# Experts in four units of columns, down parts between the units, and seven products in place of eight in two units' gates

## The chip, the core and the metric

One core of a Trainium2 chip runs the kernel. The metric is the time of one execution on the device in microseconds (us); less is better. TensorE (PE; its weight loads are PEld), VectorE (DVE), ScalarE (ACT), GpSimd (POOL) and SyncE (SP) run side by side and wait for one another through semaphores. DMA engines bring weights from HBM to SBUF, and the DMAs of one queue are served in the order of issue.

## The reference

A two-layer encoder for 256 tokens of width 1024, float32. Each layer has a mixer (a gated linear recurrence and a dilated attention) and a feed-forward part; the first layer's is a dense SwiGLU, the second's has eight experts of which each token uses two:

```python
def moe_swiglu(h, w_router, w_gate, w_up, w_down):
    logits = (h @ w_router).astype(jnp.float32)
    top_val, top_idx = lax.top_k(logits, TOP_K)
    top_w = jax.nn.softmax(top_val, axis=-1)
    combine = jnp.sum(jax.nn.one_hot(top_idx, N_EXPERTS, dtype=jnp.float32) * top_w[..., None], axis=-2)
    out = jnp.zeros(h.shape, jnp.float32)
    for e in range(N_EXPERTS):
        y = swiglu(h, w_gate[e], w_up[e], w_down[e]).astype(jnp.float32)
        out = out + combine[..., e:e + 1] * y
    return out.astype(h.dtype)
```

`swiglu` is `(silu(h @ w_gate) * (h @ w_up)) @ w_down`. Gate and up matrices are 1024 x 3584, the down matrix is 3584 x 1024, per expert. The eight experts' weights are 352 MB.

## The kernel before

Up to about 650 us the kernel does the mixers, the dense layer and the routing; the change leaves that alone. Then come the experts, one after the other, e = 0 to 7. For each, 96 places (`CAP`) hold the tokens that chose it, in three groups (`GROUPS_E`) of 32 (`STRIP`). The gathered rows, transposed, are `gT` (two buffers, by the parity of e); the next expert's rows are fetched by an indirect DMA of POOL into `fetched` and transposed by VectorE (`turn_fetched`).

**TensorE.** The token groups are the stationary operand, 32 columns wide, so four products run at once in four lanes of 32 columns of the array; a weight matrix's rows stream through. float32 products take two passes, and each pass is recorded as one weight load and one multiply, so a product has four records. The gate and up matrices are cut into two units (`UNITS_E`) of 1792 columns, 448 (`LANE_W`) per lane. A *part* is one load: for gate and up 128 rows by 1792 columns (896 KB, 12 products of 448 columns, L1508), 32 parts in an expert; for the down matrix 256 rows by 1024 columns (1024 KB, L1536), 14 parts. `E_ORDER` lists the 46 parts; the down parts come last. Gates are summed in three banks (`early`), ups in three others (`late`), the down products in `turn[0]`, `turn[1]` and `late[2]`.

**Seven products in place of eight.** In experts 0 to 6 (`seven`), two of the three token groups and each down part are treated as 2 x 2 blocks: with sums of weight blocks t1 to t4 (`sums_a`, `sums_w`, four sets, `SETS`) and sums of token blocks s1 to s4 (`xn`), seven products do the work of eight. With the third group's four, a down part has 11 products instead of 12. VectorE makes the sums: one operation of 1024 columns (t1 and t3, L2135), one of 512 (t2, "third sum", L2140, semaphore `w_second`), one of 512 (t4, "fourth sum", L2124, `w_sums`). TensorE waits for `w_second` before a down part and for `w_sums` within it. Expert 7 has the plain 12 products (L1570, L1582; of its last three parts the products into `turn[1]` come after those into `turn[0]`).

**VectorE in an expert.** Adding up the previous expert's rows and choosing the next one's (about 13 us); gating of unit 0 (L2219: up times SiLU of the gate; L2223: transposes into `hT`; L2110 to L2115: the token sums), the transposes of the next rows (L2099), the sums of the first three down parts (`AHEAD`), which stand behind a wait for those parts to land; gating of unit 1, and the sums of the other eleven. ScalarE takes the SiLU of a unit's gates (L1145).

**Loads.** SP issues one DMA per part (L742). The experts' parts go through a ring of 11 places (`RING`: `wide`, ten places that are partly `raw` before, and `extra`). Part m is asked for when part m-11 has been used. The first ten are asked for before the experts start, the eleventh (L738) when the gathered tokens are stored.

## Time and profile before

| what | value |
|---|---|
| median of 3 runs | 1529.07 us (1528.86 to 1533.36) |
| profiled execution | 1528.53 us |
| its span (first to last instruction) | 1526.7 us |
| TensorE busy | 1508.6 us, 99% |
| VectorE busy | 921.5 us, 60% |
| ScalarE busy | 497.4 us, 33% |
| HBM, read and written | 476 MB, 312 GB/s over the span |
| granted TensorE clock | 0.998 of 2.4 GHz |

The page cuts the span into 40 slices of 38.2 us; a digit is the busy share in tenths. The experts begin in the eighteenth slice. A busy TensorE isn't a TensorE at its peak, since a multiply's record covers its way through the array too; the pace is better read from the starts of pieces in the chain, the list of work that ended last. "DMA to landing" is the time from the issue of a load to the moment its semaphore is complete.

### The profile page before, as it was taken

How to read it: one execution, taken by the hardware profiler on the slowest of the kernel's cores; microseconds unless marked ns; L12 is line 12 of the kernel's file. 1: busy time of each engine (PE TensorE's matmuls, PEld its weight loads, DVE VectorE, ACT ScalarE, POOL GpSimd, SP SyncE). 2: the span in 40 equal slices, each digit the busy share in tenths (PEclk: the TensorE clock that was granted, in tenths of full speed). 3: DMA queues.
4: the chain of work that ended last, by engine and by line, in shares of the span. 5: the costliest groups of instructions: out<-in, count | busy, mean ns of one | idle time of the engine just before them, and what ended most of it. 6: DMA issues, size and time to landing. Idle time of an engine off the chain costs nothing.

```text
span 1526.7 us, 27999 instructions
## 1 busy us (share of the span) xinstructions
PE 1508.6 (99%) x11888; PEld 1033.6 (68%) x11888; DVE 921.5 (60%) x1533; ACT 497.4 (33%) x741; POOL 25.3 (2%) x39
## 2 busy tenths in 40 slices
PE   9999999999999999999999999999999999999997
PEld 7887788888888878843466566565565665664664
DVE  7778776888787776643824835726528339248211
ACT  5698745444457987420020110100100100201001
POOL 0000000000000000010000000000000000000100
PEclk9999999999999999999999999999999999999999
DMA  9544376555554444499999999999999999999994
GB/s 385 177 162 164 116 248 207 186 184 182 194 179 149 155 166 146 141 364 425 425 410 425 425 417 425 418 416 425 418 420 426 413 425 424 412 425 416 422 425 183
DMA packets 72673, 478.10 MB, mean 313 GB/s; under 512 B 8097, under 2 KB 8353, under 8 KB 45154
## 3 DMA queue, kind: packets, MB, share of 16 engines
q1 hardware_dynamic: 68656, 460.09, 75.8%
q0 software_dynamic: 3456, 15.72, 2.7%
q8 instruction: 97, 1.59, 0.4%
q10 hardware_dynamic: 434, 0.45, 0.1%
q14 instruction: 30, 0.25, 0.0%
HBM read 471.38 MB, written 4.85 MB: 312 GB/s over the span
## 4 chain that ended last, share of the span: by engine, by line
PE 85%; ACT 6%; DVE 5%; DMA 2%; issue 1%; SPq 0%; ACTq 0%; DVEq 0%
PE bank L1508 24%; PE mid L1508 12%; PE turn L1536 11%; PE bank L1233 7%; PE bank L1239 7%; PE bank L1242 7%; PE mid L1536 4%; PE mid L1233 2%; PE mid L1239 2%; PE mid L1242 2%; PE turn L1570 2%; ACT w_hi L586 1%; DVE w_lo L593 1%; DMA wide<-in_e_down 1%; PE mid L1345 1%
## 5 line engine op out<-in xcount | busy, mean ns | idle before, releaser
L1508 PE MATMUL bank<-wide,gT 128*32 128x448 f32 x3624 | 438.5, 539 | 0.0
L1508 PEld LDWEIGHTS bank<-wide,gT 128*32 128x32 f32 x3624 | 221.4, 110 | 131.6 <-issue 22.6
L593 DVE TENSOR_TENSOR w_lo<-raw,w_hi 128x1024 fp32r<-128x1024 f32 x202 | 244.4, 1223 | 93.0 <-ACT w_hi L586 90.6
L1508 PE MATMUL mid<-wide,gT 128*32 128x448 f32 x1824 | 254.2, 539 | 0.0
L586 ACT ACTIVATE w_hi<-raw 128x1024 fp32r<-128x1024 f32 (+1 forms) x202 | 210.2, 1053 | 101.1 <-PE bank L1242 65.5
L1145 ACT ACTIVATE eh<-bank 128x448 f32<-128x448 f32 x48 | 22.6, 544 | 478.3 <-PE bank L1508 478.3
L1536 PE MATMUL turn<-wide,hT 128*32 128x512 f32 x534 | 176.8, 592 | 1.4 <-DVE sums_w L2140 1.4
L1233 PE MATMUL bank<-w_hi,a_hi 128*128 128x512 f32 (+1 forms) x608 | 164.6, 394 | 0.8 <-ACT a_hi L869 0.8
L2219 DVE TENSOR_TENSOR eh<-mid,eh 128x448 f32<-128x448 f32 x32 | 19.8, 620 | 241.2 <-PE mid L1508 241.2
L1508 PEld LDWEIGHTS mid<-wide,gT 128*32 128x32 f32 x1824 | 115.5, 110 | 66.4 <-issue 12.8
L1242 PE MATMUL bank<-w_lo,a_hi 128*128 128x512 f32 (+1 forms) x608 | 157.1, 381 | 2.1 <-DVE w_lo L593 2.1
L1239 PE MATMUL bank<-w_hi,a_lo 128*128 128x512 f32 (+1 forms) x608 | 157.7, 383 | 0.0
L1536 PE MATMUL mid<-wide,hT 128*32 128x512 f32 x498 | 137.7, 592 | 0.0
L1242 PEld LDWEIGHTS bank<-w_lo,a_hi 128*128 128x128 f32 x608 | 111.3, 188 | 25.1 <-DVE w_lo L593 2.9
L1239 PEld LDWEIGHTS bank<-w_hi,a_lo 128*128 128x128 f32 x608 | 111.9, 189 | 22.7
L1233 PEld LDWEIGHTS bank<-w_hi,a_hi 128*128 128x128 f32 x608 | 109.4, 189 | 22.7 <-ACT a_hi L869 1.2
L1536 PEld LDWEIGHTS turn<-wide,hT 128*32 128x32 f32 x534 | 54.6, 109 | 56.1 <-issue 30.4
L1536 PE MATMUL turn<-wide,xn 128*32 128x512 f32 x178 | 91.1, 593 | 0.0
L2135 DVE TENSOR_TENSOR sums_a<-wide 128x1024 f32<-128x1024 f32 x49 | 59.8, 1220 | 49.8 <-DMA wide<-in_e_down 49.7
L1113 ACT ACTIVATE yt<-mid 32x512 f32<-32x512 f32 x7 | 4.1, 585 | 262.5 <-PE mid L1536 262.5
L2135 DVE TENSOR_TENSOR sums_w<-wide 128x1024 f32<-128x1024 f32 x40 | 48.8, 1220 | 47.9 <-DMA wide<-in_e_down 47.9
L1536 PEld LDWEIGHTS mid<-wide,hT 128*32 128x32 f32 x498 | 46.5, 110 | 25.2 <-issue 2.5
(313 smaller groups left out, 1985.0 us busy)
## 6 DMA issues: line engine op xcount, KB each, us to landing
wide<-in_e_in SPq DMA_DIRECT2D x227, 896.0 KB, 12.4
wide<-in_e_down SPq DMA_DIRECT2D x102, 1024.0 KB, 13.6
raw<-in_stream SPq DMA_DIRECT2D x100, 1024.0 KB, 4.8
extra<-in_e_in SPq DMA_DIRECT2D x23, 896.0 KB
extra<-in_e_down SPq DMA_DIRECT2D x10, 1024.0 KB
raw<-in_e_in SPq DMA_DIRECT2D x6, 896.0 KB, 4.5
wg<-in_gates POOLq DMA_DIRECT2D x2, 2048.0 KB, 10.5
table<-y_rows POOLq DMA_DIRECT2D x7, 384.0 KB
```

The lines of the kernel that those rows point to most:

```text
L586: nc.scalar.activation(w_hi[:, h % H, 0:n], raw[:, part % R, lo:lo + n], ACT.Copy).then_inc(hi_ready, 1)
L593: nc.vector.tensor_tensor(w_lo[:, h % H, :], raw[:, part % R, lo:lo + HALF], w_hi[:, h % H, :].bitcast(F32), ALU.subtract).then_inc(lo_rea ...
L1145: nc.scalar.activation(eh[t_][:, :], early[t_][:, 0:LANE_W], ACT.Silu).then_inc(e_silu, 1)
L1233: nc.tensor.matmul(o_, s_hi[:, kt, t], w_hi[:, h % H, w], start=kt == 0, stop=False)
L1239: nc.tensor.matmul(o_, s_lo[:, kt, t], w_hi[:, h % H, w], start=False, stop=False)
L1242: ins = nc.tensor.matmul(o_, s_hi[:, kt, t], w_lo[:, h % H, w], start=False, stop=kt == last_kt)
L1345: ins = nc.tensor.matmul(mid[:, q, g * T:(g + 1) * T], wg[:, d, g, n, :], xc[:, n, :], start=True, stop=True)
L1508: ins = nc.tensor.matmul((early, late)[m][t_][strip(r), 0:LANE_W], gT[:, kt, strip(t_)], w_[:, r * LANE_W:(r + 1) * LANE_W], start=kt == 0 ...
L1536: return nc.tensor.matmul(bank_[strip(lane), :], h_, b_, start=d == from_, stop=d == to)
L1570: ins = nc.tensor.matmul(turn[0][strip(s_), :], h_[:, c * CAP + STRIP * t_: c * CAP + STRIP * (t_ + 1)], w_c, start=first and c == 0, stop ...
L2135: nc.vector.tensor_tensor(own_[:, 0:2, :], blocks[:, :, 1, :], blocks[:, 0, :, :], ALU.subtract).then_inc(w_first, 1)
L2219: nc.vector.tensor_tensor(eh[t_][:, :], late[t_][:, 0:LANE_W], eh[t_][:, :], ALU.mult).then_inc(e_hid, 1)
```

## The change

- Columns: four units of 1024, 1024, 1024 and 512 columns (`WIDTHS` = 256, 256, 256, 128 per lane). Every part is now 1024 KB: two blocks of 128 rows by 1024 columns, or in unit 3 four blocks of 128 rows by 512. An expert has 28 gate and up parts and 14 down parts, 42 loads in place of 46, from one tensor `e_parts`.
- Order in an expert (parts counted from 0): unit 0 (0 to 7), unit 1 (8 to 15), down parts of unit 0 (16 to 19), unit 2 (20 to 27), down of unit 1 (28 to 31), unit 3 (32 to 35), down of unit 2 (36 to 39), down of unit 3 (40, 41). In units 0 to 2 two gate parts, two up parts, two gate parts, two up parts.
- Gates of units 1 and 2 in experts 0 to 6 have seven products in place of eight for two token groups: 28 products of 128 columns and, for the third group, 8 of 256. The other parts have 24 products of 256 columns; in unit 3 they have 48 of 128.
- The weight sums of these 8 gate parts per expert are made by VectorE like those of the down parts, in the same four sets and with the same lead of three parts: 22 parts in place of 14. The seven gate products are then combined: ScalarE copies two of them out of PSUM, VectorE makes five additions (`combine_gate`), ScalarE takes the SiLU of the result. Four more operations of 128 columns per expert sum the gathered rows (`gathered_sums`).
- VectorE's program in an expert follows the parts: in step i the sums of part i+3, the fourth sum of a part behind the first of the next; the combination and the gating of a unit at the step in which its last gate or up part has been used; the transposes of the next rows in steps 9, 10 and 11.
- The products of the ups use `late[0]` and `late[1]` only, so `late[2]`, `turn[0]` and `turn[1]` are taken by the down products from part 16 on.

```diff
-UNITS_E = 2
-LANE_W = F_EXP // (UNITS_E * LANES)
+WIDTHS = (256, 256, 256, 128)
+UNITS_E = len(WIDTHS)
+LANE_W = WIDTHS[0]
+SEVEN_UNITS = (1, 2)
...
+    return unit(0) + unit(1) + down(0) + unit(2) + down(1) + unit(3) + down(2) + down(3)
...
+                        act.wait_ge(used, u0 + GATE_END[u] + e * E_PARTS)
+                        if split:
+                            k = len(SEVEN_UNITS) * e + SEVEN_UNITS.index(u)
+                            nc.scalar.activation(part_sum[:, 0, :], early[0][:, 0:P], ACT.Copy).then_inc(gate_copied, 1)
+                            nc.scalar.activation(part_sum[:, 1, :], early[1][:, 2 * P:3 * P],
+                                                 ACT.Copy).then_inc(gate_copied, 1)
...
+                                four(early[0][:, 0:P], a11, b11, opens=True)
+                                four(early[0][:, P:2 * P], a12, b21)
+                                four(early[1][:, 0:P], s4, b22, opens=True)
+                                pe.wait_ge(w_second, n + 1)
+                                four(early[1][:, 3 * P:4 * P], s3, t3)
+                                four(early[1][:, 2 * P:3 * P], s1, t1)
+                                four(early[0][:, 2 * P:3 * P], s2, t2, closes=True)
+                                pe.wait_ge(w_sums, n + 1)
+                                four(early[1][:, P:2 * P], a22, t4, closes=True).then_inc(w_sums_used, 1)
...
+                        for i in range(E_PARTS):
+                            if i in UP_END or i in GATE_END and GATE_END.index(i) in SEVEN_UNITS:
+                                if owed is not None:
+                                    fourth_sum(e, owed)
+                                    owed = None
+                                if i in UP_END:
+                                    gating(e, UP_END.index(i))
+                                else:
+                                    combine_gate(e, GATE_END.index(i))
+                            if 9 <= i < 9 + GROUPS_E:
+                                turn_fetched(e, [i - 9])
+                            if i + AHEAD in SEVENS:
+                                first_sums(e, i + AHEAD)
+                                if owed is not None:
+                                    fourth_sum(e, owed)
+                                third_sum(e, i + AHEAD)
+                                owed = i + AHEAD
+                                if i + 1 + AHEAD not in SEVENS:
+                                    fourth_sum(e, owed)
+                                    owed = None
```

`four` issues one product of 128 columns in each of the four lanes.

TensorE before, in expert 0, from the end of the third down part to the fourth and into the fifth (`turn0`, `turn1` and `mid` are the down sums, `xn` the token sums, `part_landed` a load's semaphore, `weight_sums_third` is `w_second`, `weight_sums_ready` is `w_sums`):

```order
L1536 MATMUL turn0<-sums_w,hT 32x512 [waits weight_sums_ready]
L1536 MATMUL mid<-wide,hT 32x512 x2
L1536 MATMUL turn0<-wide,hT 32x512 [waits weight_sums_third,part_landed1]
L1536 MATMUL turn1<-sums_w,xn 32x512 x2
L1536 MATMUL turn0<-sums_w,xn 32x512
L1536 MATMUL turn1<-wide,hT 32x512
```

TensorE after, in expert 0, from the end of the down parts of unit 0 into the first gate part of unit 2 and to the next one (`gS` holds the sums of the gathered rows, `bank0` to `bank2` the gates):

```order
L1602 MATMUL turn0<-sums_w,hT 32x512 [waits weight_sums_ready]
L1602 MATMUL mid<-wide,hT 32x512 x2
L1542 MATMUL bank0<-wide,gT0 32x128 [waits gathered_sums,expert_silu,part_landed9]
L1542 MATMUL bank0<-wide,gT0 32x128 x7
L1542 MATMUL bank1<-wide,gS 32x128 x4
L1542 MATMUL bank1<-sums_a,gS 32x128 [waits weight_sums_third]
L1542 MATMUL bank1<-sums_a,gS 32x128 x7
L1542 MATMUL bank0<-sums_a,gS 32x128 x4
L1542 MATMUL bank1<-sums_a,gT0 32x128 [waits weight_sums_ready]
L1542 MATMUL bank1<-sums_a,gT0 32x128 x3
L1558 MATMUL bank2<-wide,gT0 32x256 x8
L1542 MATMUL bank0<-extra,gT0 32x128 [waits part_landed10]
```

Down parts now end in gate parts of the same expert, and a gate part has a second wait for VectorE's sums in its middle.

VectorE before, in expert 0, from the end of the gating of unit 1 to the sums of the fourth and fifth down part:

```order
L2113 TENSOR_TENSOR xn<-xn,hT 128x224 [waits hidden_sums]
L2115 TENSOR_TENSOR xn<-hT,xn 128x224 [waits hidden_sums]
L2135 TENSOR_TENSOR sums_a<-wide 128x1024 [waits weight_sums_used,part_landed3]
L2140 TENSOR_TENSOR sums_a<-sums_a,wide 128x512 [waits weight_sums_first_pair]
L2135 TENSOR_TENSOR sums_w<-wide 128x1024 [waits weight_sums_used,part_landed4]
```

VectorE after, in expert 0, from the combination of unit 1's gates over the sums of parts 17 and 18 and the gating of unit 1 to the sums of part 19 (`gs` is the combined gate, `eh` the gated values):

```order
L2214 TENSOR_TENSOR gs<-bank1,part_sum 128x256 [waits gate_sums_steps]
L2243 TENSOR_TENSOR sums_a<-wide 128x1024 [waits weight_sums_used,part_landed6]
L2251 TENSOR_TENSOR sums_a<-sums_a,wide 128x512 [waits weight_sums_first_pair]
L2243 TENSOR_TENSOR sums_w<-wide 128x1024 [waits weight_sums_used,part_landed7]
L2259 TENSOR_TENSOR sums_a<-wide,sums_a 128x512 [waits weight_sums_third]
L2251 TENSOR_TENSOR sums_w<-sums_w,wide 128x512 [waits weight_sums_first_pair]
L2259 TENSOR_TENSOR sums_w<-wide,sums_w 128x512 [waits weight_sums_third]
L2224 TENSOR_TENSOR eh<-bank3,eh 128x512 [waits expert_silu,halves_used]
L2226 TENSOR_TENSOR eh<-mid,eh 128x256 [waits expert_silu]
L2229 STREAM_TRANSPOSE hT<-eh 128x8x32 [waits expert_hidden] x3
...
L2243 TENSOR_TENSOR sums_w<-wide 128x1024 [waits weight_sums_used,part_landed8]
```

The sums of two of the next four down parts stand ahead of the gating and need those parts' landing; those of the fourth stand behind it.

## Rows read from the trace of the kernel before

**Rows 1.** From the page: span, busy times, DMA's busy tenths by slice.

```profile
span 1526.7 us, 27999 instructions
PE 1508.6 (99%) x11888; PEld 1033.6 (68%) x11888; DVE 921.5 (60%) x1533; ACT 497.4 (33%) x741; POOL 25.3 (2%) x39
DMA  9544376555554444499999999999999999999994
```

**Rows 2.** Windows: length, each engine's busy us (records), PE clock, DMA share, GB/s.

```profile
660.00:670.00 10.00, 10.00 (x108) 3.94 (x110) 8.75 (x45) 1.77 (x2) 2.12 (x3) 1.00 0.77 301
...
690.00:700.00 10.00, 10.00 (x112) 3.51 (x108) 2.88 (x6) 1.42 (x3) 0.00 (x0) 1.00 1.01 422
...
845.00:855.00 10.00, 10.00 (x90) 3.88 (x84) 9.96 (x14) 0.00 (x0) 0.00 (x0) 1.00 1.02 430
```

**Rows 3.** The chain that ended last, in order of time: start us, length us, what.

```profile
767.31 4.88 PE bank L1508 x51
...
839.47 2.80 PE turn L1536 x26
...
873.64 4.89 PE bank L1508 x51
...
1507.54 5.15 PE turn L1570 x48
```

**Rows 4.** Timeline of VectorE and TensorE: first down part of experts 0 and 6; expert 7.

```profile
719.32 1.23 DVE L2135 TENSOR_TENSOR sums_a<-extra 128x1024 f32<-128x1024 f32 x1 [11.98 <-DMA extra<-in_e_down]
...
1363.49 1.23 DVE L2135 TENSOR_TENSOR sums_a<-wide 128x1024 f32<-128x1024 f32 x1 [18.01 <-DMA wide<-in_e_down]
...
732.94 0.59 PE L1536 MATMUL turn<-extra,hT 128*32 128x512 f32 x1
...
1370.38 0.59 PE L1536 MATMUL turn<-sums_a,xn 128*32 128x512 f32 x1
...
1405.84 0.56 PE L1508 MATMUL bank<-wide,gT 128*32 128x448 f32 x1
```

**Rows 5.** SP's loads (L742): windows 660:700, 1450:1490, 1382.5:1384.6, and its timeline.

```profile
DMA to landing us min/median/max: 7.2/9.1/9.8
...
L742 SPq DMA_DIRECT2D wide<-in_e_down x13: 327/328/328, 1456.7 to 1487.0; - x13
...
DMA to landing us min/median/max: 18.6/19.8/20.7
...
DMA to landing us min/median/max: 14.2/15.1/15.9
...
1382.73 0.44 SPq L742 DMA_DIRECT2D wide<-in_e_in  x1
```

**Rows 6.** Timeline of weight loads at expert 1's fourth down part: idle time in brackets.

```profile
846.25 0.14 PEld L1536 LDWEIGHTS turn<-wide,hT 128*32 128x32 f32 x2 [0.83 <-issue]
846.29 0.15 PEld L1536 LDWEIGHTS turn<-sums_a,xn 128*32 128x32 f32 x6
```

**Rows 7.** Timeline of VectorE, expert 6: gating of unit 0, sums of down parts.

```profile
1335.25 0.63 DVE L2219 TENSOR_TENSOR eh<-mid,eh 128x448 f32<-128x448 f32 x1 [23.11 <-PE mid L1508]
...
1339.92 1.36 DVE L2099 STREAM_TRANSPOSE gT<-fetched 32x256 f32<-32x256 f32 x3
...
1379.27 1.22 DVE L2135 TENSOR_TENSOR sums_a<-wide 128x1024 f32<-128x1024 f32 x1
...
1381.61 1.22 DVE L2135 TENSOR_TENSOR sums_a<-wide 128x1024 f32<-128x1024 f32 x1
```

**Rows 8.** POOL's timeline and the page's DMA issues: fetching the next expert's rows.

```profile
781.13 0.93 POOL L820 DMA_INDIRECT fetched<-tokens,index  x1 [4.87 <-DVE index L2207]
...
fetched<-tokens,index POOLq DMA_INDIRECT x7, 9.0
```

**Rows 9.** The page's instruction queue; the attention's product among groups by form.

```profile
q8 instruction: 97, 1.59, 0.4%
...
L1395 PE MATMUL turn<-pt,v 128*64 128x128 f32 x128 | 8.8, 279 | 0.0
```

More of the change, by code:

```diff
@@ L282 @@
 STATIC_PARTS = N_HALF // 2
-assert E_PARTS % SLOW == 0 and LANE_W % STRIP == 0 and UNIT_W <= PART
+assert E_PARTS % SLOW == 0 and LANES * sum(WIDTHS) == F_EXP
 WIDE = R + H
@@ L392, in build @@
             fetched = keep("fetched", [P, D], into=m)
-            eh = [keep(f"eh{i}", [P, LANE_W], into=m) for i in range(GROUPS_E)]
-            hT = keep("hT", [P, UNITS_E * UNIT_TILES, CAP], into=m)
+            eh = keep("eh", [P, GROUPS_E, LANE_W], into=m)
+            gs = keep("gs", [P, 2, LANE_W], into=m)
+            keep("gs_end", [P, 64], into=m)
+            hT = keep("hT", [P, sum(TILES), CAP], into=m)
             with ExitStack() as m2:
@@ L1503, in experts @@
[L1503 to L1512 removed]
+                            u, m, p = which
@@ new lines, in experts @@
+                            up = (late[0][:, 0:w], late[0][:, LANE_W:LANE_W + w], late[1][:, 0:w])
+                            place = [early[t_][:, 0:w] for t_ in range(GROUPS_E)] if m == 0 else up
+                            kts = PART // (LANES * w)
+                            if w == LANE_W:
+                                own_ = w_.rearrange("p (k n r c) -> p k r n c", k=kts, n=2, r=LANES)
+                            else:
+                                own_ = w_.rearrange("p (k r c) -> p k r c", k=kts, r=LANES)
@@ new lines, in experts @@
+                            for k in range(kts):
+                                kt = kts * p + k
+                                for t_ in range(GROUPS_E):
+                                    for r in range(LANES):
+                                        ins = nc.tensor.matmul(place[t_][strip(r), :], gT[:, kt, strip(t_)],
+                                                               own_[:, k, r], start=kt == 0 and (m, t_) != (1, 1),
+                                                               stop=kt == KT - 1 and (m, t_) != (1, 0))
+                        else:
+                            d = which[0]
+                            if d == 0 and pas:
@@ L1528, in experts @@
+                            first, last = d == 0, d == N_DOWN - 1
+                            if seven(pas, e):
+                                n = len(SEVENS) * e + SEVENS.index(i)
+                                if d in FIRST_DOWN:
+                                    pe.wait_ge(h_sums, 4 * (q0 + u + 1) + e * (4 * UNITS_E))
+                                pe.wait_ge(w_second, n + 1)
+                                t1, t3, t2, t4 = (set_of(n)[:, j, :] for j in range(4))
                                 s1, s2, s3, s4 = (sT[:, j, d, :] for j in range(4))
@@ L2234, in experts @@
-                    if pas and not is_last(pas, e):
-                        dve.wait_ge(used, U0 + pas * E_LAST + N_IN + e * E_PARTS)
-                        turn_fetched(e)
+                    if seven(pas, e):
+                        gathered_sums(e)
+                        owed = None
[6 more added lines that the diff above has]
+                                    gating(e, UP_END.index(i))
+                                else:
+                                    combine_gate(e, GATE_END.index(i))
[9 more added lines that the diff above has]
+                                    fourth_sum(e, owed)
+                                    owed = None
+                    else:
+                        for u in range(UNITS_E):
+                            if is_last(pas, e) and u == UNITS_E - 1:
+                                add_picked()
+                            gating(e, u)
+                        if not is_last(pas, e):
+                            turn_fetched(e)
```

277 lines of the change are left out of this document (161 added, 116 removed).

## The prediction

> **What bounds the kernel now.** The page comes first [rows 1]: TensorE is busy 99% of the span and VectorE 60%, and from about 660 us on the DMA engines show 9 tenths in every slice. That makes two candidates in the expert stage. By the windows [rows 2] the DMA share is 0.77 between 660 and 670 and 1.01 to 1.02 later, at 422 to 430 GB/s: from 670 on the DMA engines are never empty. By the chain [rows 3] expert 1 starts at 767.31, its down parts at 839.47, expert 2 at 873.64: 106.33 us, of which 72.16 for 32 parts of the first matrices (2.255 each) and 34.17 for 14 parts of the second (2.44 each). TensorE is what ends last.
>
> The two are compared through VectorE, which waits once per expert for the landing of the first down part [rows 4]: until 719.32 in expert 0 and until 1363.49 in expert 6, 107.36 us per expert over six. TensorE reaches the same part at 732.94 and 1370.38, 106.24 us per expert. So DMA is already the slower of the two, by 1.1 us per expert, and TensorE lives on a cushion: that part lands 13.6 us before its use in expert 0 and 6.9 in expert 6. The time from issue to landing says the same, median 9.1 us from 660 to 700 and 18.6 to 20.7 after 1450 [rows 5]. The last load is issued at 1487.0, so it lands near 1507; its first use is the last of the three groups of turn[0] that begin at 1507.54 and take 5.15 together [rows 3], that is at 1511.0. Only 4 us are left there.
>
> **TensorE's work, part by part.** In a lane a product is two passes. 12 products of 448 columns in four lanes are 6 passes in 2.255 us, 0.3758 each; the 24 products of 512 columns at 1507.54 are 12 passes in 5.15, 0.429 each [rows 3]. From the two: 0.834 ns per column and 2 ns per pass, so 0.109 us for 128 columns and 0.216 for 256.
> - Unit 0, and the up parts of units 1 and 2: 24 products of 256 columns, 12 passes, 2.590 us; 16 such parts are 41.4.
> - A gate part with seven products: 28 products of 128 and 8 of 256, 14 and 4 passes, 2.389 us; 8 are 19.1.
> - Unit 3: 48 products of 128, 24 passes, 2.616 us; 4 are 10.5.
> - Together 71.0 against 72.16, 1.15 less. The last expert, which has no seven products, has 72.6, 0.46 more.
> - A down part has 11 products, 5.5 passes, 2.361 us; 14 are 33.05 against 34.17. The 1.1 us between are waits: TensorE's weight loads stand 0.83 us before 846.25 [rows 6], where VectorE, late from the gating of 448 columns, ends the third sum of the fourth down part. Most of this should go, since a unit's gating becomes shorter and is spread.
>
> **VectorE's new work.** The sums of one part take 2.34 us (1379.27 to 1381.61, [rows 7]); 8 more parts are 18.7 us per expert. Gating a unit with its transposes and sums takes 4.7 us (1335.25 to 1339.92) for 448 columns; with some 0.07 us per operation and a column per 1.04 ns (1.22 us for 1024 columns, 0.63 for 448, same rows) 256 columns give 3.0, the five combining steps 1.5, the sums of the gathered rows 1.0. VectorE idles 40% now; place, not amount, decides. I walk the place where unit 1 meets the first down parts, t=0 at the end of its last gate part (part 13 of an expert). ACT copies two products until 0.6, VectorE combines until 2.0, has the sums of parts 17 and 18 at 7.1, has gated unit 1 at 10.1 and has the third sum of part 19 at 12.0. TensorE has two up parts until 5.2, then parts 16 to 18, and wants part 19 at 12.3. It fits with 0.3 us to spare. Behind the wait for the combination stand ACT's SiLU and all of VectorE's sums; behind the gating, the sums of part 19, for which TensorE waits. I allow 0.5 us of waits per expert, between none and the whole gain of 2.3. The transposes of the next expert's rows now stand behind the gating of unit 0, some 24 us into an expert; the rows are asked for 13.8 us into it and take 9 [rows 8], so they have just landed: nothing, or 1 to 2 us per expert if they are late.
>
> So TensorE alone would need about 104.6 us per expert in place of 106.3: seven times 1.7, less 0.5 in the last, 11 us.
>
> **DMA's work.** The weights' bytes stay. Three things move. The ring's first ten places are filled before the experts start, and a place now takes 1024 KB, not 896: 1.31 MB, at 423 GB/s 3.1 us earlier for all that follows, since DMA has room before 670 [rows 2]. Rows of 8 KB in place of 7 KB: 430 GB/s with down parts in flight, 422 with the others [rows 2], though such windows scatter; at 0.5% of 70 us that is 0.4 us less per expert. And instructions: 864 products per expert, not 384, with 4 records each, are 1920 more; 1.59 MB for 23,776 records is 67 bytes each, 8 packets more, and 0.4% of 1527 us for 97 packets is 0.063 us each [rows 1, 9], 0.5 us more per expert. The last two cancel: DMA keeps its 107.4, within 1 us.
>
> **What is late next.** TensorE would eat 2.8 us of the cushion per expert (107.4 minus 104.6). Seven products need a part earlier than TensorE does. From the walk: part 18 lands S before its use, then come 3.2 us of sums, 3.0 of gating and 1.9 for the third sum of part 19, which is wanted 2.4 after part 18; S must be 5.7. At the end of expert 0 the cushion is 13.6 plus 3.1 less 1.2, and it falls to 5.7 in about expert 4. From there VectorE makes TensorE wait until 5.7 is there again, and experts run at 107.4. So DMA sets the gain. Expert 7's first part, issued at 1382.73 and landed at most 15.9 us later, 1398.6, was used at 1405.84 [rows 4, 5]. Now it lands at 1395.5 and is used with what TensorE's faster last parts leave of S, about 5.5, at 1401.0: 4.8 less. With 0.46 more in expert 7, and 0.2 for a ring that starts later behind larger first loads, 4.1 us remain. The last part then lands at 1504 and is wanted at 1507: no second wait.
>
> **Forecast.** The profiled execution took 1528.5 (span 1526.7 and 1.8 around it), half a microsecond under the median of the three runs, 1529.07. 4.1 less than the median is **1525.0**. Bounds of this case: S of 4.7 or 7 is 1 us either way; only half of DMA's 3.1, 1527.
>
> **Rivals.**
> - *Only the last landing binds.* If VectorE sums and gates faster than walked, the cushion can go to nothing: 3.1 plus 4.0, 7.1 us, 1522.0. Against it stand durations that hardly vary [rows 7].
> - *The saved product is lost in waits.* If combining, gating or the gathered rows cost TensorE 2.3 us per expert, it stays at 106.3 and the time is 1529 to 1530. For it: the walk leaves 0.3 us, and the wait of 0.83 us is of this kind.
> - *Small products are not fed fast enough*, the case that ends slower. In unit 3 four lanes want 8 records (load and multiply) in 0.107 us, 13.4 ns each. The densest stretch of before is the attention's product in two lanes, 128 multiply records in 8 groups in 8.8 us [rows 9]: 1.1 us per group, less 0.28 for its last record, is 0.12 per pass and four records, 29 ns each, where the array may be the limit itself. So 13.4 is shown by no row. At r ns per record unit 3 takes 768 r per expert and the gate parts 1152 r. From 16.2 ns on unit 3 costs 2.0 us more than walked, and the kernel is 0.3% slower; at 17 ns it is 3.1 us, seven times (3.1 minus 1.7), 2.6 in the last expert and its 0.5: 13 us, 1542. At 27 ns it would be 1680. For a good outcome: after the wait in [rows 6] six loads start within 0.15 us.
> The Trainium skill (Runtime: NRT & Kernel Launch, Instruction fetch mechanics) gives an issue floor of about 20 cycles per instruction, and with the sequencer's 1.2 GHz (TensorE: Matmul & The Clock Gate, Wait — 56ns, not 53.3ns?) that is 16.7 ns per record and an estimate of 1538 here; the second page also says that matmul and weight load go straight to the engine, at about 25 ns from one small matmul to the next, which would be just enough. No row here decides between them.
> - *VectorE falls behind.* 22 parts at 2.34 and the rest are 85 of 105 us. With 10% more per operation each part of a run of sums would come 0.2 us later than wanted and gating 0.5: 1 to 3 us per expert over DMA's pace, 1540. Little speaks for it.
>
> **How the numbers follow.** DMA-bound with the walked cushion 0.46; only the last landing 0.17; lost in waits 0.15; small products 0.15; VectorE behind 0.04; unforeseen DMA time of over 1 us per expert 0.03. Below 0.3%, 4.6 us, a measurement of this kernel can't tell a change from none; faster begins at 1524.5. The forecast lies 0.5 us from that, so 0.20 of the first case counts as faster with the second: 0.37. Same: 0.26 of it and the third, 0.41. Slower: 0.22. The range takes the second case and the fourth at its 17 ns: 1520 to 1542.
>
> **What would show it.** Right: TensorE at 104 to 105 us per expert in 1 to 3 and about 107 in 5 and 6; a gate part of 2.39 us, one of unit 3 of 2.62; in the late experts VectorE's first sums wait for DMA, and TensorE for the third sum of the fourth down part. Wrong: unit 3 above 2.8 us per part (the feed); long waits for VectorE in experts 1 to 3; a cushion under 4 us in expert 6; or a DMA period far from 107.4.

## The result, and the profile after the change

The changed kernel takes **1580.76 us** (median of six runs, 1580.15 to 1584.62) against 1530.06 for the kernel before in the same session (1528.86 to 1535.30). The ratio is 1.033, with a 95% interval of 1.0310 to 1.0349. The forecast was 1525.0 with a range up to 1542, so the sign and the size are both wrong: the kernel lost some 50 us. Ratios below are to the kernel before in the run's own session, with their 95% interval.

The page of the changed kernel first: span and instructions, busy times, the DMA row, the instruction queue, the chain's shares, and the costliest group of matrix products with its weight loads. The first number behind a group's second bar is the idle time that stood before it.

```profile
span 1582.7 us, 43527 instructions
PE 1519.2 (96%) x19376; PEld 1147.5 (72%) x19376; DVE 1100.0 (70%) x1919; ACT 507.9 (32%) x803; POOL 25.4 (2%) x39
DMA  9444465555544445699999999999999999999992
GB/s 384 170 148 160 137 238 198 186 203 198 180 166 145 137 157 186 261 413 407 380 414 404 361 410 394 383 423 369 393 419 351 406 414 375 411 424 358 419 425 104
...
q8 instruction: 156, 2.56, 0.6%
...
PE 84%; ACT 6%; DVE 4%; issue 4%; DMA 1%; ACTq 0%; DVEq 0%; POOLq 0%
...
L1574 PE MATMUL bank<-wide,gT 128*32 128x256 f32 (+1 forms) x6448 | 388.4, 346 | 30.5 <-issue 30.4
L1574 PEld LDWEIGHTS bank<-wide,gT 128*32 128x32 f32 x6448 | 264.1, 111 | 101.2 <-issue 42.3
...
wide<-in_e_parts SPq DMA_DIRECT2D x300, 1024.0 KB, 9.6
```

Beside [rows 1] TensorE is no longer busy 99% but 96% of a longer span. Of its idle time 30.4 us stand before one group and end in "issue": the engine waited for nothing that the profile shows. A load lands 9.6 us after its issue at the median, less than the 12.4 us or more of the kernel before, and the rate falls to 351 to 380 GB/s in single slices. So the weights aren't what is late.

The windows of expert 1, cut at its stages, show where the time is. The columns are length, busy us and records of TensorE's products, of its weight loads, of VectorE, ScalarE and GpSimd, then the granted clock, the DMA share and GB/s. The rows are unit 0, unit 1, the first four down parts, unit 2, the next four, unit 3, and the last six.

```profile
772.76:794.04 21.28, 21.28 (x393) 20.84 (x389) 14.00 (x34) 7.87 (x15) 1.49 (x2) 1.00 1.02 406
794.04:814.72 20.68, 20.48 (x488) 17.36 (x482) 19.20 (x38) 1.35 (x4) 0.00 (x0) 1.00 1.01 411
814.72:825.12 10.40, 9.62 (x92) 2.94 (x88) 10.26 (x19) 0.00 (x0) 0.00 (x0) 1.00 1.01 425
825.12:847.73 22.61, 20.58 (x482) 17.21 (x478) 15.98 (x24) 1.35 (x4) 0.00 (x0) 1.00 1.01 422
847.73:857.17 9.44, 9.44 (x95) 2.92 (x91) 8.84 (x17) 0.00 (x0) 0.00 (x0) 1.00 0.99 386
857.17:874.26 17.09, 12.45 (x391) 11.88 (x387) 4.16 (x6) 0.62 (x3) 0.00 (x0) 0.93 0.96 379
874.26:888.55 14.29, 14.29 (x137) 5.28 (x132) 9.15 (x18) 0.00 (x0) 0.00 (x0) 0.96 0.75 292
```

The walked times were 20.72, 19.92, 9.44, 19.92, 9.44, 10.46 and 14.17. Unit 3 has 6.6 us more than walked, unit 2 has 2.7, unit 1 has 0.8, unit 0 has 0.6, the first down parts 1.0. At 4.3 us, a part of unit 3 is far over the 2.8 that the prediction named as the sign of a feed that is too slow. Expert 1 takes 115.8 us; the mean of experts 0 to 6 is 113.9, where 104.6 was forecast for TensorE alone and 107.4 for DMA. The chain of waits inside unit 3:

```profile
857.45 5.99 PE bank L1574 x207
863.44 2.42 issue
865.86 0.43 PE mid L1574 x8
...
869.56 2.23 issue
871.78 1.06 PE bank L1574 x16
```

Two idle stretches of 2.4 and 2.2 us. Between them TensorE's timeline counts 128 multiplies in its groups of 8 and 16, and as many weight loads go with them: 256 instructions. The DMA view says what happens beside each stretch. These are its rows for the instruction queue (packets, MB, share of the 16 DMA engines) in two windows, 863.6 to 864.7 and 869.4 to 870.4; there is none from 864.7 to 869.4.

```profile
q8 instruction: 1, 0.02, 5.4%
...
q8 instruction: 1, 0.02, 5.5%
```

A packet of that queue is 2.56 MB over 156, 16.4 KB. It carries 256 instructions (the 256 of the trace; that is 64 bytes each). The first packet starts at 863.66, lasts 0.95 us, and TensorE goes on at 865.86, 1.25 us after its end; the next starts at 869.46, ends at 870.33, and TensorE goes on at 871.78. It is so everywhere: of TensorE's stops of over 0.4 us that are put to issue from 690 us on, all 30 end between 1.2 and 1.6 us behind the end of such a packet. So TensorE had run out of instructions. That is the theory from here on, **the feed**: instructions come through the DMA engines in blocks of 256, here 5.8 us from one to the next beside full weight loads, and unit 3 wants one every 3.4 us. Where TensorE stops twice in a row at full clock, the two packets start 5.7 to 6.5 us apart (eight such pairs). The trace shows the coincidence; that the feed is the cause needs runs.

The clock adds a part. The window of 872 to 873 us in the same unit, right behind the two stretches:

```profile
872.00:873.00 1.00, 1.00 (x25) 1.00 (x21) 0.00 (x0) 0.00 (x0) 0.00 (x0) 0.50 0.95 401
```

The granted clock is 0.50, 1.2 GHz, until about 875.3. In the table above unit 3 has a clock of 0.93 and the stage behind it 0.96, together 1.7 us of lost clock.

### The profile page after: what moved, and what is told of

It reads as the page before. It is cut to its first block, busy times and chain, and to the rows that moved or that the text cites. A ratio compares the mean times of both kernels' runs of the same rounds, so it can differ in the third digit from the quotient of the medians.

```text
span 1582.7 us, 43527 instructions
## 1 busy us (share of the span) xinstructions
PE 1519.2 (96%) x19376; PEld 1147.5 (72%) x19376; DVE 1100.0 (70%) x1919; ACT 507.9 (32%) x803; POOL 25.4 (2%) x39
## 3 DMA queue, kind: packets, MB, share of 16 engines
q8 instruction: 156, 2.56, 0.6%
## 4 chain that ended last, share of the span: by engine, by line
PE 84%; ACT 6%; DVE 4%; issue 4%; DMA 1%; ACTq 0%; DVEq 0%; POOLq 0%
PE bank L1574 21%; PE turn L1602 11%; PE bank L1259 7%; PE bank L1265 7%; PE bank L1268 7%; PE mid L1574 6%; PE bank L1542 5%; PE mid L1602 4%; PE bank L1558 3%; PE mid L1259 2%; PE mid L1265 2%; PE mid L1268 2%; PE turn L1634 2%; ACT w_hi L603 1%; PE mid L1371 1%
## 5 line engine op out<-in xcount | busy, mean ns | idle before, releaser
L1574 PE MATMUL bank<-wide,gT 128*32 128x256 f32 (+1 forms) x6448 | 388.4, 346 | 30.5 <-issue 30.4
L1574 PEld LDWEIGHTS bank<-wide,gT 128*32 128x32 f32 x6448 | 264.1, 111 | 101.2 <-issue 42.3
L1574 PE MATMUL mid<-wide,gT 128*32 128x256 f32 (+1 forms) x1808 | 192.6, 360 | 6.2 <-issue 6.1
L1602 PE MATMUL turn<-wide,hT 128*32 128x512 f32 x546 | 186.0, 595 | 0.8 <-DVE sums_a L2251 0.8
L2224 DVE TENSOR_TENSOR eh<-bank,eh 128x512 f32<-128x512 f32 (+1 forms) x32 | 19.9, 622 | 179.4 <-PE mid L1574 179.4
L1265 PEld LDWEIGHTS bank<-w_hi,a_lo 128*128 128x128 f32 x608 | 111.9, 189 | 22.7
L1574 PEld LDWEIGHTS mid<-wide,gT 128*32 128x32 f32 x1808 | 96.9, 113 | 28.0 <-issue 8.7
L1172 ACT ACTIVATE eh<-bank 128x256 f32<-128x256 f32 (+1 forms) x68 | 19.4, 343 | 270.8 <-PE bank L1574 270.8
L2243 DVE TENSOR_TENSOR sums_w<-wide 128x1024 f32<-128x1024 f32 x71 | 86.5, 1218 | 0.3
L2243 DVE TENSOR_TENSOR sums_a<-wide 128x1024 f32<-128x1024 f32 x71 | 86.5, 1218 | 0.3
L1558 PE MATMUL bank<-wide,gT 128*32 128x256 f32 x816 | 64.9, 380 | 2.6 <-issue 2.4
```

Source lines behind the costliest of these rows:

```text
L1265: nc.tensor.matmul(o_, s_lo[:, kt, t], w_hi[:, h % H, w], start=False, stop=False)
L1558: ins = nc.tensor.matmul(early[2][strip(r), 0:w], h_, own_[:, k, r, :, :], start=p == 0 and k == 0, stop=p == KT // 2 - 1 and k == 1)
L1574: ins = nc.tensor.matmul(place[t_][strip(r), :], gT[:, kt, strip(t_)], own_[:, k, r], start=kt == 0 and (m, t_) != (1, 1), stop=kt == KT - ...
L1602: return nc.tensor.matmul(bank_[strip(lane), :], h_, b_, start=d == from_, stop=d == to)
L2224: nc.vector.tensor_tensor(eh[:, 0:2, 0:w], both[:, :, 0:w], eh[:, 0:2, 0:w], ALU.mult).then_inc(e_hid, 2)
L2243: nc.vector.tensor_tensor(own_[:, 0:2, :], blocks[:, :, 1, :], blocks[:, 0, :, :], ALU.subtract).then_inc(w_first, 1)
```

## Experiments

**Is it DMA that slows the feed?** The first run leaves every instruction in place and takes the load off the DMA engines.

```
-                load_expert(place_of(PLACE[m]), PLACE[m], m % E_PARTS, m // E_PARTS)
+                if m < 3 * RING:
+                    load_expert(place_of(PLACE[m]), PLACE[m], m % E_PARTS, m // E_PARTS)
+                else:
+                    source, _ = expert_part(m % E_PARTS, m // E_PARTS)
+                    sp.dma_start(place_of(PLACE[m])[:, 0:CB // 2], source[:, 0:CB // 2]).then_inc(landed[PLACE[m]], 16)
```

> The changed kernel, but from the 34th part of the ring on (three turns of it) each load of an expert part brings only 256 of its 2048 columns, so the products multiply stale weights and the output is not the reference's; instructions, order and waits are the same. The feed theory says that TensorE runs out of instructions because their 16 KB blocks stand in DMA engines full of weights: unit 3 then falls from 16 to 22.7 us to about 10.5 us (its array time), the idle times of TensorE in the stage put down to issue fall from about 10 us per expert to below 1, and an expert takes 103 to 106 us in place of 114. A rival, that TensorE's sequencer or queue can't issue such small products faster whatever DMA does, keeps unit 3 at 16 us and an expert at 112 or more. A second rival, that the landings of the weights are late, also gives about 105 us, but then the idle time would be put down to DMA in the kernel with full loads, and the gaps would not follow the instruction packets.

It took 1529.2 us (one run). The windows are the first down parts of expert 1, its unit 3, and unit 3 of expert 3:

```profile
810.00:820.76 10.76, 9.81 (x95) 5.68 (x90) 10.62 (x20) 0.00 (x0) 0.00 (x0) 1.00 0.13 37
...
850.25:861.49 11.24, 10.66 (x388) 10.47 (x384) 5.20 (x7) 0.61 (x3) 0.00 (x0) 1.00 0.23 63
...
1062.64:1073.27 10.63, 10.63 (x387) 10.42 (x383) 5.20 (x7) 0.62 (x3) 0.00 (x0) 1.00 0.26 65
```

Unit 3 falls from 17.1 us to between 10.5 and 11.3 in the experts with light loads. A limit in TensorE or its sequencer on so short products would have stayed; it is out. In 10.63 us go 768 instructions, 13.8 ns each, less than the 16.2 ns from which the prediction's rival began to cost anything. The run takes load off the DMA engines, HBM and SBUF at once, so it shows that the load slows the feed, and not at which of them an instruction packet waits. The experts take 106.1 us each on average (769.72 to 1406.44 for six), not the 104.1 of the array: 1.3 of it is the wait for VectorE at the first down parts, 10.76 us in place of 9.44. That is the place that the prediction walked with 0.3 us to spare. It shows here, where nothing else is late.

**Which part of the change asks too fast?** Three kernels undo one or both of the dense pieces. In the first, a gate column block and its up block of unit 3 stand side by side in one product of 256 columns.

```
-                            kts = PART // (LANES * w)
+                            kts = 2
...
+                                place = [early[t_][:, 0:2 * w] for t_ in range(GROUPS_E)]
```

> The changed kernel with gate and up columns of unit 3 side by side in one product of 256 columns: 96 products in unit 3 in place of 192, the same columns, everything else as in the changed kernel. Feed theory: unit 3 takes its array time, 10.4 us in place of 16; the gate parts with seven products (288 instructions behind 288 in a row) still wait 1 to 2 us per unit; 6 us per expert come back, 1530 to 1540 us. Rival (VectorE late behind the shared seven-product sums, or DMA landing late): unit 3 shortens, but the wait comes back at the down parts behind it, and the time stays above 1565.

> As the pairs in unit 3, and eight products in the gates of units 1 and 2 in place of seven: no gate sums on VectorE, no product under 256 columns, 672 products per expert in place of 864. Feed theory: no instruction block is asked for sooner than every 6.9 us, no idle time put down to issue over 0.5 us; an expert takes the 107.4 us that DMA needs, or 105.6 where TensorE sets it, 1524 to 1529 us. Rival (units in four and down parts between them cost by themselves, through gating, transposes or waits for the landings): above 1540.

The second adds this line to the first; the third has this line alone, with the call for the sums of the gathered rows taken out in both:

```
-SEVEN_UNITS = (1, 2)
+SEVEN_UNITS = ()
```

> The changed kernel with eight products in the gates of units 1 and 2, unit 3 left as it is (192 products of 128 columns in 10.5 us of array time). Only unit 3 then asks for instructions faster than they came in the starved stretches (256 per 3.4 us against 5.8). Feed theory: units 1 and 2 take 20.7 us each without a gap, unit 3 takes 15 to 16 us, 5 us over its array time; an expert takes about 110.5 us, 1555 to 1562 in all, so that the 50 us that the change lost are parted into about 25 from unit 3 here and 15 to 20 from the seven-product gates of the kernel with pairs in unit 3. If the loss lay in VectorE's work for the seven-product gates, 1530 to 1535.

They took in turn 1538.9 us (1.0056, 1.0038 to 1.0075), 1530.3 (1.0007, 0.9997 to 1.0016) and 1559.2 (1.0204, 1.0183 to 1.0224). Unit 3 with pairs, in expert 1 of the first, and units 2 and 3 of expert 3 in the kernel without seven-product gates:

```profile
851.18:861.54 10.36, 10.36 (x196) 10.36 (x192) 5.24 (x7) 0.00 (x0) 0.00 (x0) 1.00 1.02 426
```

```profile
1042.65:1063.52 20.87, 20.87 (x389) 13.31 (x385) 7.47 (x9) 0.94 (x3) 0.00 (x0) 1.00 1.01 424
1072.82:1087.79 14.97, 11.47 (x393) 10.73 (x389) 5.55 (x7) 0.61 (x3) 0.00 (x0) 1.00 1.01 425
```

The places are those that the feed theory named. With half the instructions for the same columns unit 3 takes its array time under full loads; without the seven-product gates unit 2 has no gap, and the kernel with pairs and without those gates has not one stop of over 0.4 us put to issue. Against the kernel with neither, the small products of unit 3 alone cost 28.9 us, the seven-product gates alone 8.6, and both 50.5 (30, 7.5 and 49 by the ratios, since the sessions differ). The 8.6 is under the 15 to 20 that I had parted off for them, and the kernel with neither is 1 us above its expected 1524 to 1529. They cost more together than apart; DMA limits the kernel with neither (below), so each alone can hide in part behind it, which was not tested by itself.

**Is it the instructions, or how densely they stand?** The next kernel keeps all instructions and transfers of the changed one and changes the order of parts.

```
-    return unit(0) + unit(1) + down(0) + unit(2) + down(1) + unit(3) + down(2) + down(3)
+    return (unit(0) + unit(1) + unit(2)[:4] + down(0) + unit(2)[4:] + unit(3)[:2] + down(1) + unit(3)[2:]
+            + down(2) + down(3))
```

> The changed kernel, every instruction and every transfer kept, in another order of parts: the first four down parts stand in the middle of unit 2 in place of ahead of it, the next four between unit 3's gate and its up parts. A down part wants 44 instructions in 2.36 us, so a run of dense parts is cut to 480 instructions in 10 us and 384 in 5.2 us, with 9.4 us of slow parts behind each. Feed theory (about 256 instructions per 5.8 us come whatever is asked, with at least one block held ahead): units 2 and 3 lose at most 1 to 2 us per expert together, unit 1 still 1 to 2; 3 to 5 us per expert come back, 1540 to 1560 us. A fixed limit on how fast small products issue once the instructions are there would keep unit 3 at 16 us and the time at 1575 to 1585.

1555.9 us (1.0174, 1.0157 to 1.0191): half of the loss is back with the same instructions. The windows are units 0, 1 and half of 2; the other half of 2 with the gate of 3; and the up parts of 3.

```profile
772.32:826.34 54.02, 51.52 (x1106) 44.16 (x1104) 44.68 (x91) 9.22 (x19) 1.50 (x2) 1.00 1.01 414
835.78:853.70 17.92, 15.68 (x438) 14.41 (x434) 11.39 (x23) 1.35 (x4) 0.00 (x0) 1.00 1.01 417
862.94:868.42 5.48, 5.48 (x196) 5.34 (x192) 0.88 (x2) 0.00 (x0) 0.00 (x0) 1.00 0.99 381
```

Array time is 50.6, 15.2 and 5.2 us. The up parts, as dense as before but with 9.4 us of down parts ahead, have 0.3 us over it. What is left stands where dense parts follow each other, 3.4 us in the long run and 2.7 in the second. I had expected 1 to 2 for unit 1, and half of unit 2 now stands in the same run; the rest of units 2 and 3 loses 3.0 where 1 to 2 were expected. The total is in its range.

**Does the row size matter?** The host lays out the two halves of a part apart, so that a load goes in 4 KB rows.

```
-            return e_parts[e * E_PARTS + i, :, :], PART
+            return e_parts[e * E_PARTS + i, :, :, :].rearrange("h p c -> p h c"), PART
```

> The changed kernel with the experts' weights stored in two halves of 1024 columns, so that a load of 1 MB goes in 256 descriptors of 4 KB and not 128 of 8 KB: same bytes, same order. If an instruction packet waits behind a fixed number of weight descriptors in its DMA engine, that wait (3.6 of the 5.8 us between two starved blocks) halves, a block comes every 4 us, unit 3 falls to 12 or 13 us, and the kernel takes 1545 to 1560 unless smaller rows cost DMA bandwidth (1% of it is 1 us per expert). If the wait is one for bytes or has nothing to do with the queue, 1578 to 1590.

1574.5 us (1.0294, 1.0277 to 1.0312), 6 us less than the changed kernel and far from what half the wait would give; neither expected range, 1545 to 1560 or 1578 to 1590, holds it. In expert 2 unit 3 takes 15.1 us, where it took 16.3 in the changed kernel:

```profile
969.99:985.10 15.11, 11.34 (x391) 10.81 (x387) 4.28 (x7) 0.62 (x3) 0.00 (x0) 1.00 1.02 401
```

Between two stops in a row at full clock, a packet starts 3.5 to 3.8 us after TensorE went on, against 3.4 to 4.2 in the changed kernel. With rows of half the size the wait did not halve, so it isn't one for a fixed number of rows. What it is in the engines stays open.

**How fast can the feed be, and where is the edge?** These runs start from the kernel before, with its products of 448 columns cut into four of 112 (start and stop flags on the first and last cut), and then with nearly idle DMA engines as in the first experiment, after five turns of the ring. `CUT` is 112.

```
+                                for c_ in range(0, LANE_W, CUT):
+                                    for r in range(LANES):
+                                        ins = nc.tensor.matmul((early, late)[m][t_][strip(r), c_:c_ + CUT],
```

> The kernel before, with each product of 448 columns of the experts' first matrices cut into four of 112: the same columns and the same result, 1536 products per expert in place of 384 in that phase, 6144 instructions at four each. Array time by the law of 0.834 ns per column and 2 ns per pass: 192 x 4 x 0.0954 = 73 us in place of 72. Feed theory: at 256 instructions per 5.8 us (22.7 ns each, as in the starved stretches of the changed kernel) the phase takes 139 us, an expert about 173 us, and the kernel some 2050 us. If small products cost only their array time, 1530 to 1545 us.

> The kernel before with its first products cut in four (the earlier experiment), and each load from the 56th part of the ring on (five turns) with 256 of its columns only, so the output is not the reference's. Feed theory: with the DMA engines nearly idle the 6144 instructions of a first phase, 106 to 115 us under full loads, take their array time of about 73 us from expert 2 on, or what unloaded fetches allow if that is less than 256 per 3.05 us; the kernel ends near 1570. A limit in TensorE or its sequencer leaves the phase at 106 to 115 us and the time above 1800.

1836.9 and 1682.8 us (one run each). The first phase of expert 1 with full loads, and of expert 3 with light ones:

```profile
801.35:912.70 111.35, 84.12 (x3072) 79.58 (x3070) 25.52 (x55) 9.78 (x18) 1.48 (x2) 0.94 0.82 297
```

```profile
1053.36:1139.30 85.94, 78.21 (x3073) 73.07 (x3071) 25.44 (x55) 9.77 (x18) 1.47 (x2) 1.00 0.23 62
```

With 24 blocks in a phase that is 4.6 us per block in the first and 3.6 in the second (3.6 to 3.7 over its five experts with light loads). Both expectations of the feed missed in size. The first said 5.8 us per block. Since the ring waits for TensorE here, the DMA share is only 0.82, and a block waits less: the price of a block goes with what DMA is doing. The granted clock of 0.94 isn't what sets the 4.6, since packets between which it was 1.00 start 4.8 us apart on average. The second said that the phase would shrink to its 73 us of array time. It did not: it shows the turn of one block, from one to the next, with little else on the DMA engines. The timeline of TensorE with light loads:

```profile
1201.88 0.67 PE L1514 MATMUL bank<-wide,gT 128*32 128x112 f32 x18 [0.47 <-issue]
...
1205.62 1.44 PE L1514 MATMUL mid<-wide,gT 128*32 128x112 f32 x50 [0.47 <-issue]
...
1209.64 0.67 PE L1514 MATMUL bank<-wide,gT 128*32 128x112 f32 x18 [0.75 <-issue]
```

By the DMA records packets start at 1203.02 and 1206.74: 1.1 us after TensorE goes on, 1.0 and 1.4 us for the packet, 1.5 until TensorE goes on again, 3.7 to 4.0 in all; the mean of this phase is 3.6. It looks as if one block is asked for at a time, when TensorE enters the last one it has. In the starved unit 3 of the changed kernel a packet starts 3.6 us after TensorE went on (865.86 to 869.46) in place of 1.1: 2.5 us more beside full weight loads. Cut in two, not four, a block is wanted every 6.1 us:

> The kernel before, each product of 448 columns cut into two of 224: 3072 instructions in an expert's first phase in place of 1536, one block of 256 per 6.1 us of array time (192 x 2 products in 73 us), full loads. Feed theory, with a loaded block every 5.7 to 6.2 us where TensorE waited for each: demand and supply are about even, so the phase takes 73 to 76 us and the kernel 1530 to 1550; the cut in four, at one block per 3.05 us, lost 38.5 us per expert. If time went by the number of instructions and not by a rate that is passed (a third of the 4608 instructions that the cut in four adds, a third of its loss), 12.8 us per expert, 1631.

1540.6 us (1.0068, 1.0048 to 1.0088), and a first phase at its array time:

```profile
769.13:841.60 72.47, 72.47 (x1535) 51.88 (x1533) 25.52 (x55) 9.77 (x18) 1.48 (x2) 1.00 1.02 417
```

So the feed has an edge: at one block per 6.1 us of array time nothing is lost in the phase, at 3.05 us the phase takes half as long again. Yet the kernel is 11 us slower, and the list of waits (us, times, longest) says for whom. The first row is VectorE's longest wait for weights; the others are all of TensorE's from 660 to 1510 us.

```profile
DVE sums_a L2138 <- DMA wide<-in_e_down: 57.4, 7, 19.5
...
PE turn L1539 <- DVE sums_w L2143: 2.5, 2, 1.3
PE turn L1539 <- DVE sums_a L2143: 2.2, 2, 1.6
PE bank L1510 <- issue: 0.4, 1, 0.4
```

The kernel before has this row for VectorE:

```profile
DVE sums_a L2135 <- DMA wide<-in_e_down: 49.7, 7, 18.0
```

VectorE waits longer for weights, and TensorE then for VectorE's sums, hardly for issue. By packets and bytes only the instruction queue grew on the DMA engines, 145 packets in place of the 97 of [rows 9]; the weights' own packets took a little longer too (75.4% of 1539.2 us in place of 75.8% of 1526.7, some 3 to 4 us). By the medians the kernel takes 11.4 us more with 48 more blocks, 0.24 us each. Half of the dose, with only the gate products cut, asks whether that is so:

> The kernel before with only the gate products cut into two of 224 columns: 768 more instructions in an expert's first phase, three blocks of 16 KB, 24 in all, half of the dose of the cut in two of all products. That one took 11.4 us more with 48 more blocks, its phase of 72.5 us without a gap, its VectorE waiting for DMA, and 414 to 416 GB/s moved where the kernel before moves 421 at the same full DMA share: 0.24 us of DMA time per block. If a block costs DMA that much, 5.7 us more, 1534 to 1536. If a block costs what its packet takes of sixteen engines (0.063 us), 1.5 us more, 1530 to 1531.5, and the lower rate with all products cut has another cause.

1534.1 us (1.0026, 1.0015 to 1.0037), by the interval 2.3 to 5.7 us for 24 blocks, where the packets alone ask for 1.5. The 48 blocks cost 7.3 to 13.5 us by theirs. Taken as the blocks' doing, which rests on these two doses, that is 0.1 to 0.28 us for each, up to some four times the 0.063 that its packet takes of sixteen engines. Why is open: the trace does not say which of the sixteen engines carries the instruction packets.

**What is left without the feed's loss?** Two kernels combine the remedies: pairs in unit 3 and the spaced order, and the same with seven products in unit 2 only.

```
-SEVEN_UNITS = (1, 2)
+SEVEN_UNITS = (2,)
```

> The changed kernel with both remedies: gate and up columns of unit 3 in one product of 256, and the first eight down parts put between halves of unit 2 and of unit 3. It keeps the seven-product gates, so TensorE's array time is 104.1 us per expert, under the 107.4 to 108 that DMA needs. Feed theory: only the densest stretch left, unit 1 (960 instructions in 19.9 us, one block per 5.3 us), loses 1 to 2 us per expert at times, which DMA's period hides in the later experts; then the rest of the prediction is seen bare: experts at DMA's pace, 1525 to 1533 us. If the seven-product gates cost something by themselves through VectorE (its sums make the last one late in the kernel with light loads), up to 1540.

> As the kernel with pairs and spaced down parts, but seven products only in the gate of unit 2 and eight in unit 1, so that no more than half a unit with seven products stands in a row (480 instructions in 10 us, with 9.4 us of down parts behind the first half and pairs behind the second). TensorE's array time is 104.9 us per expert. Feed theory: the 3.5 us of idle time per expert that stood in the run of unit 1 and half of unit 2 shrink below 0.5, TensorE is faster than DMA's 107.4 to 107.9 and DMA alone sets the time: 1524 to 1530, the cushion of VectorE's sums deciding between them. If the idle time stays above 2 us per expert, it was not the dense run of unit 1 that made it, and the time is 1533 to 1540.

1540.1 us (1.0068, 1.0052 to 1.0083) and 1534.7 (1.0025, 1.0010 to 1.0041), both above what the feed theory said. The windows of the first, expert 1: units 0, 1 and half of 2; four down parts; the rest of 2 and the gate half of 3; four down parts; and the other half of 3.

```profile
768.60:822.93 54.33, 51.68 (x1105) 43.88 (x1103) 44.32 (x91) 9.22 (x19) 1.50 (x2) 1.00 1.01 416
822.93:832.37 9.44, 9.44 (x93) 5.13 (x89) 6.67 (x9) 0.00 (x0) 0.00 (x0) 1.00 0.98 396
832.37:847.52 15.15, 15.15 (x341) 11.82 (x337) 8.50 (x19) 1.35 (x4) 0.00 (x0) 1.00 1.00 413
847.52:856.96 9.44, 9.44 (x94) 5.13 (x90) 9.37 (x13) 0.00 (x0) 0.00 (x0) 1.00 1.01 424
856.96:862.14 5.18, 5.18 (x101) 3.70 (x97) 3.40 (x5) 0.00 (x0) 0.00 (x0) 1.00 1.02 429
```

All stages but the long first one run at their array time. That one has 3.7 us over its 50.6, and TensorE's 104.1 us become 107.8. The spaced order removed one run of dense parts and made another longer. With seven products in unit 2 alone the long run is at array time, as expected, and another wait appears. The windows are that run in expert 1, and the second four down parts in expert 4:

```profile
766.40:817.81 51.41, 51.41 (x1010) 49.60 (x1008) 31.78 (x73) 8.80 (x18) 1.49 (x2) 1.00 1.01 415
1160.04:1172.52 12.48, 9.79 (x96) 3.73 (x92) 10.58 (x19) 0.00 (x0) 0.00 (x0) 1.00 1.01 419
```

Those down parts take 12.48 us in place of 9.44, with VectorE waiting for DMA landings ahead of them. Early experts take 105.2 us, later ones 107 to 109: the cushion is eaten and DMA sets the pace, which the prediction had described, with 41 more instruction blocks on it than in the kernel before. No version of the four-unit kernel that was run beats the kernel before; the nearest, pairs without seven-product gates, can't be told from it.

## Why the prediction was wrong

**The step that failed** is the one on instructions in "DMA's work". It found the 1920 more instructions per expert and the 8 more packets, and priced them by their bytes: 0.5 us per expert of DMA time. How long a block takes to arrive stood in no term. From one block to the next it is 3.6 to 3.7 us with nearly idle DMA engines and 5.7 to 6.5 with full ones, one at a time as far as the trace shows, and unit 3 uses one up in 3.4. So unit 3 took 17.09 us for the 10.46 walked, and expert 1 took 115.8 for 104.1. Two rows could have raised the question: the rate (256 instructions at the 13.4 ns that the prediction itself computed), and the 9 us and more that a load takes to land in the full queues [rows 5].

**The rival "small products are not fed fast enough"** had the right stage and the right sign, at a chance of 0.15; the range took it at 17 ns only, up to 1542. Its mechanism was a price per record, r, the same at any place. By that law the 17.09 us of unit 3 (22.3 ns per record) would have cost the gates 6.6 us per expert as well, and made some 1617 in all; units 1 and 2 together lost 3.5 in expert 1. The law is one of blocks: nothing is lost while a run of dense parts lives on what is held ahead, then the rate of the feed rules until a sparse part comes. And it changes with the load on DMA, which a price per record can't.

The Trainium skill (Runtime: NRT & Kernel Launch, Instruction fetch mechanics) describes the blocks, 256 instructions of 64 bytes fetched by the sequencer's own DMA queue while the page before is executed, and this trace agrees: 256 instructions between two packets of 16.4 KB. It calls the cost of passing from one block to the next "mostly hidden" and says that the issue floor hides the fetch; here the trace disagrees, with 30.4 us of idle time in one group alone. The prediction took the floor from that section and passed over the fetch.

**TensorE's walk** was right wherever it was fed: 10.36 us for unit 3 in pairs, 15.15 for half of unit 2 and half of unit 3 (9.96 and 5.18 walked), 9.44 for four down parts.

**VectorE's tight place** was sized at 0.5 us per expert and measures 1.3 where DMA is nearly idle, 1.0 in expert 1 of the changed kernel. In expert 1 of the kernels with the spaced order the first four down parts take 9.44 us: there it costs nothing.

**DMA's 107.4 us per expert** held within its bound of 1 us for the kernel without dense pieces (107.8 and 108.3 in experts 5 and 6 of the pairs without seven-product gates). But that kernel, with nothing starved, takes 1530.3 us, 5 more than the forecast, so the 4.1 us of gain would probably have been missed even with the feed in order. An estimate: its 36 more blocks, at 0.1 to 0.28 us each and not 0.063, are 3.6 to 10 us, as much as the 3.1 of the earlier start of the ring and more; no run took this apart.

**The clock** was in no sum. It fell to 0.50 behind two idle stretches of 2.4 and 2.2 us and took 1.7 us more from expert 1.

## What to carry to other kernels

Before cutting products smaller, divide 256 by the instructions per microsecond that each run of parts asks for. Compare it with the time from one instruction block to the next under the load that DMA has there (3.6 to 3.7 us nearly idle, 5.7 to 6.5 full in this kernel). The sum over an expert can be harmless while one stage in it starves: here 1018 products of four instructions in 107 us are 26 ns each, slower than the 22.7 of the starved stretches. A transfer has two prices, its bytes and its delay; in a kernel whose DMA queues are kept full on purpose, whatever else goes through them pays the second. Where the same columns can go in fewer and wider products, or dense parts between sparse ones, the loss comes back without any change of the arithmetic.

## What the runs showed of the hardware

- TensorE's instructions come in blocks of 256, in packets of 16.4 KB that the profile counts among those of the 16 DMA engines. With nearly idle engines a starved block comes every 3.6 to 3.7 us, of which the packet is 1.0 to 1.4; with a DMA share of 0.82 every 4.6 on the average of a phase, with full loads every 5.7 to 6.5.
- A starved TensorE goes on 1.2 to 1.6 us after a packet's end, with light loads or full ones. What grows with the load is the time from its going on to the next packet's start, from 1.1 to 3.6 us.
- 4 KB rows in place of 8 KB change that little: 3.5 to 3.8 us in place of 3.4 to 4.2, and the kernel is 6 us of 1580 faster.
- With light loads 768 instructions of TensorE go in 10.63 us, 13.8 ns each.
- In the DMA-bound kernel, 24 more instruction blocks went with 2.3 to 5.7 us more and 48 with 7.3 to 13.5: 0.1 to 0.28 us each, more than the 0.063 that a packet takes of sixteen engines.
- In expert 1, stops of TensorE of 2.4 and 2.2 us were followed by a granted clock of 0.50 (1.2 GHz) from 872 to about 875.3 us. A pair of 1.7 and 2.2 us in expert 0 was not: the clock stayed at 1.00.
